# Attention of a two-layer diffusion step: another order for value matmuls, prompt items, inverse sums and modulation chunks

## The reference

```python
def block_attention(q, k, v):
    ...
    def one_block(qi):
        s = jnp.einsum('bqhd,bkhd->bhqk', qi, k).astype(jnp.float32) * scale
        p = jax.nn.softmax(s, axis=-1).astype(v.dtype)
        return jnp.einsum('bhqk,bkhd->bqhd', p, v)
...
def layer_step(x, mod, rope, ctx_ckv, ctx_krope, p):
    sh1, sc1, g1, sh2, sc2, g2 = jnp.split(mod, 6, axis=-1)
    h = rmsnorm(x, p['norm1_g']) * (1 + sc1) + sh1
    mix, ckv, kpe = token_mixers(h, rope, ctx_ckv, ctx_krope, p)
    x = x + g1 * mix
    ...
mod_lat = (jax.nn.silu(c) @ w_ada[l] + b_ada[l])[:, None, :]
```

## Time and profile before

| what | us |
|---|---|
| median of three runs | 2453.25 |
| lowest and highest of them | 2451.75, 2464.22 |
| the profiled execution | 2446.93 |
| its span, first to last instruction | 2445.2 |
| mean granted TensorE clock in it, as a share of full speed | 0.977 |

### The profile page before, as it was taken

How to read it: one execution, slowest core, us unless ns; L and a number is a source line. 1 busy time by engine, 2 the same in 40 slices (tenths; PEclk the granted TensorE clock), 3 DMA queues, 4 the chain that set the end, 5 groups by cost and what they waited for, 6 DMA issues and landing times.

```text
span 2445.2 us, 30291 instructions
## 1 busy us (share of the span) xinstructions
PE 2318.5 (95%) x12256; PEld 1512.7 (62%) x12256; DVE 748.3 (31%) x1419; ACT 508.0 (21%) x1048; POOL 276.9 (11%) x434
## 2 busy tenths in 40 slices
PE   6999989999997999999999999999999969999996
PEld 4545546555445887888754455455554458887884
DVE  2401245553338111111142022545623541111113
ACT  3310122221334101010142102212223320111003
POOL 3000011211001112111210000220100011112111
PEclk8999999999998999999999999999999979999998
DMA  9100169768246888889950001975642268888888
GB/s 335 34 6 16 52 133 248 203 124 233 95 154 224 263 276 271 274 279 287 327 166 17 22 0 52 204 171 114 128 125 103 78 241 275 269 273 283 274 279 296
DMA packets 215864, 440.44 MB, mean 180 GB/s; under 512 B 31936, under 2 KB 75128, under 8 KB 215776
## 3 DMA queue, kind: packets, MB, share of 16 engines
q1 hardware_dynamic: 167920, 358.71, 46.6%
q0 software_dynamic: 22768, 54.29, 9.0%
q10 hardware_dynamic: 25088, 26.23, 4.7%
HBM read 339.08 MB, written 47.65 MB: 158 GB/s over the span
## 4 chain that ended last, share of the span: by engine, by line
PE 77%; issue 7%; DMA 6%; DVE 4%; ACTq 1%; POOL 1%; ACT 1%; SPq 1%; POOLq 0%; DVEq 0%
PE PS L1361 11%; PE PS L1368 11%; PE PS L1207 11%; PE PS L1393 9%; PE PS L991 8%; PE PS L945 6%; PE PS L932 5%; PE PS L1387 2%; PE PS L1084 2%; DMA inv_dram<-oinv 2%; PE PS L1141 2%; ACTq L1587 1%; PE PS L1096 1%; PE PS L1045 1%; DMA r<-ring 1%
## 5 line engine op out<-in xcount | busy, mean ns | idle before, releaser
L1361 PEld LDWEIGHTS PS<-r,ring 128*128 128x128 f32 x2048 | 281.9, 190 | 15.2 <-issue 15.2
L1207 PE MATMUL PS<-ring,mix 128*128 128x512 f32 x640 | 288.4, 598 | 1.2 <-DVE mix L1966 1.2
L1361 PE MATMUL PS<-r,ring 128*128 128x160 f32 x2048 | 284.0, 299 | 0.3 <-ACT r L1687 0.3
L1368 PE MATMUL PS<-r,ring 128*128 128x160 f32 x2048 | 283.4, 299 | 0.0
L1368 PEld LDWEIGHTS PS<-r,ring 128*128 128x128 f32 x2048 | 279.9, 190 | 0.0
L1393 PE MATMUL PS<-ring,r 128*128 128x512 f32 x496 | 221.1, 599 | 0.0
L991 PE MATMUL PS<-r,ring 128*128 128x512 f32 (+1 forms) x576 | 208.4, 521 | 1.6 <-ACT r L1485 1.6
L1084 PE MATMUL PS<-lat,r 128*128 128x512 f32 (+1 forms) x416 | 191.2, 595 | 15.0 <-ACT ring L1550 7.1
L1141 PE MATMUL PS<-r 128*128 128x256 f32 x768 | 183.3, 391 | 15.3 <-DMA r<-ring 9.8
L1207 PEld LDWEIGHTS PS<-ring,mix 128*128 128x128 f32 x640 | 116.4, 190 | 129.7 <-issue 129.7
L1141 PEld LDWEIGHTS PS<-r 128*128 128x128 f32 x768 | 147.4, 195 | 59.9 <-issue 18.0
(11 more groups left out here) (308 smaller groups left out, 2176.1 us busy)
## 6 DMA issues: line engine op xcount, KB each, us to landing
ring<-in_w_gate_dram SPq DMA_DIRECT2D x32, 2048.0 KB
ring<-in_w_up_dram SPq DMA_DIRECT2D x32, 2048.0 KB, 11.6
ring<-in_w_down_dram SPq DMA_DIRECT2D x31, 2048.0 KB, 9.4
ring<-in_w_ada_dram SPq DMA_DIRECT2D x15, 2048.0 KB, 9.9
r<-ring SPq DMA_DIRECT2D x128, 96.0 KB
r<-ring ACTq DMA_DIRECT2D x128, 96.0 KB
r<-r SPq DMA_DIRECT2D x128, 96.0 KB
r<-r ACTq DMA_DIRECT2D x128, 96.0 KB
```

Of the source, the lines that this page charges most:

```text
L1207: ins = pe.matmul(psum(2 * (s % 2) + n, 512), mix[:, k, tile * P:(tile + 1) * P], W_OUT[n][:, k, :], start=(k == 0), stop=(k == KD - 1))
L1361: ins = pe.matmul(PS[:, b // 2, (b % 2) * 256:(b % 2) * 256 + SLOTS], W_G[:, k, b * P:(b + 1) * P], XST[par][:, k, :], start=(k == 0), sto ...
L1368: ins = pe.matmul(PS[:, 2 + b // 2, (b % 2) * 256:(b % 2) * 256 + SLOTS], W_U[:, k, b * P:(b + 1) * P], XST[par][:, k, :], start=(k == 0), ...
```

## The change

Six edits, all in the attention stage and the first steps of the projection:

1. `ITEMS`: both prompt items come last, as items 16 and 17.
2. TensorE's loop: all of `times_values(n - 2)` stands behind the scores of item n. `modulation(n)` follows it, and `turn_modulation(n - 1)` stands behind the first scores of item n. So chunk i belongs to item i, from iteration 0 on.
3. SP: two modulation loads ahead of the first exchange, later ones behind the exchange of the item two before.
4. VectorE's loop: `copy_modulation(n - 1)` first, `divide_out(n - 4)`, `invert_sums(n)` and `bias_modulation(n)` last.
5. `INV`, `oinv` and `inv_dram` have four buffers instead of two, and the last item's inverse goes through DRAM as the others do; `spread_last`, `divide_last` and the matmul with ones are gone. POOL's store for the last item stands behind its loads of the gates.
6. Value heads: eight matmuls of 512 columns for the sample tokens between the last value matmuls, and the four of 256 columns for the prompt tokens (`prompt_value_heads`) in the second step of the projection.

```diff
@@ -45,8 +45,8 @@
 for _p in range(2):
-    ITEMS.append((_p, PROMPT_TILES))
     ITEMS += [(_p, t) for t in range(PT, NT)]
+ITEMS += [(_p, PROMPT_TILES) for _p in range(2)]
...
-        INV = [lat[:, 512 * i:512 * (i + 1)] for i in range(2)]
-        DIAG = lat[:, 1024:1280].rearrange("p (s q) -> p s q", s=2)
+        INV = [lat[:, 512 * i:512 * (i + 1)] for i in range(4)]
...
@@ -530,16 +528,18 @@
+                load_ada(0)
+                load_ada(1)
                 for n in range(NI):
-                    if n < len(ADA_ITEMS[l]):
-                        load_ada(n)
+                    exchange(n, (0, 1))
+                    if n + 2 < len(ADA_ITEMS[l]):
+                        load_ada(n + 2)
...
-                    exchange(n, (0, 1))
@@ -712,21 +712,21 @@
                 def spread_inverses(n):
...
-                    if l + n:
-                        pool.wait_ge(inv_landed, at(l, 16 * (NI - 1), 16 * n))
+                    if n >= 4:
+                        pool.wait_ge(inv_landed, at(l, 16 * NI, 16 * (n - 3)))
...
-                    if n >= 2:
-                        pool.wait_ge(o_divided, at(l, NI, n - 1))
+                    if n >= 4:
+                        pool.wait_ge(o_divided, at(l, NI, n - 3))
...
                 for n in range(NI - 1):
-                    store_gate(n - 2)
+                    store_gate(n)
                     spread_inverses(n)
...
+                spread_inverses(NI - 1)
...
@@ -1144,56 +1145,54 @@
                     for c in range(3):
                         scores(n, 0, c)
-                    modulation(n - 2)
-                    times_values(n - 2, first_half)
+                    turn_modulation(n - 1)
                     if n:
                         pe.wait_ge(exp_done, at(l, 2 * NI, 2 * n))
...
-                    turn_modulation(n - 2)
-                    times_values(n - 2, second_half)
+                    times_values(n - 2, range(12))
+                    modulation(n)
 
                 n = NI - 1
+                pe.wait_ge(o_divided, at(l, NI, 8))
+                value_heads(0)
+                value_heads(1)
                 pe.wait_ge(exp_done, at(l, 2 * NI, 2 * n + 1))
...
+                value_heads(2)
+                value_heads(3)
                 times_values(n - 1, range(12))
                 pe.wait_ge(exp_done, at(l, 2 * NI, 2 * n + 2))
...
                 pe.wait_ge(o_divided, at(l, NI, 12))
+                value_heads(4)
+                value_heads(5)
+                pe.wait_ge(o_divided, at(l, NI, 16))
+                pe.wait_ge(uvh_copied[0], at(l, NU // 2, 1))
                 value_heads(6)
+                pe.wait_ge(uvh_copied[1], at(l, NU // 2, 1))
                 value_heads(7)
...
-                pe.matmul(psum(6, 256), ones[:, :], DIAG, start=True, stop=True).then_inc(inv_summed, 1)
...
                 times_values(n, range(12))
...
@@ -1289,6 +1291,10 @@
                 for s in range(NT):
+                    if s == 1:
+                        pe.wait_ge(o_divided, at(l, NI, NI))
+                        prompt_value_heads(0)
+                        prompt_value_heads(1)
                     project(s, 0, 0)
...
                 for n in range(NI):
-                    bias_modulation(n - 2)
-                    divide_out(n - 3)
+                    copy_modulation(n - 1)
                     row_max(n, 0)
                     row_max(n, 1)
-                    copy_modulation(n - 2)
                     turn_blocks(n, 0)
                     turn_blocks(n, 1)
-                    if n < NI - 1:
-                        invert_sums(n)
+                    divide_out(n - 4)
+                    invert_sums(n)
+                    bias_modulation(n)
```

113 lines of the change are left out of this document (45 added, 68 removed).

## The result

| kernel | median, us | runs | profiled span, us | granted clock | first attention, us | second attention, us |
|---|---|---|---|---|---|---|
| before | 2455.28 | 17 | 2445.2 | 0.977 | 269.2 | 267.5 |
| changed | 2462.69 | 17 | 2460.9 | 0.972 | 271.5 | 272.4 |
| forecast for changed | 2430.5 | | | | 259.2 | 250.4 |

The ratio of changed to before is 1.0038, with a 95% interval of 1.0022 to 1.0054: slower by a little, within 0.5% at the median, and far outside the range of 2417 to 2445 us. An attention is counted, as in the prediction, from its first score matmul to its first output projection. The prediction's 252.6 us for the second holds 2.2 us of prompt value heads that lie behind that end, so 250.4 stands in the table.

The account below looks back on a forecast made before the run. TensorE, 95% busy, was taken as the bound, with time to win only where it stands. Summed stage times gave gains of 7.8 and 14.9 us, 22.7 in all: 2453.25 becomes 2430.5 us, range 2417 to 2445.

Parts of the forecast that it names:

- Values at the end: Attention loop: all value matmuls at the iteration's end give exchanges more time; their waits go, 0 in the full loop.
- all fit into 20.9: Attention loop: exchanges measured at 10.8, 17.8 and 17.9 us land within the 20.9 us from issue to first value matmuls.
- The load order: SP queue: modulation loads have 24.6 us from issue to use, as before; no wait was counted.
- Rival 4: Modulation iterations: DMA backlog from iterations 0 and 1 makes 8 iterations wait; 13 us slower, 2466.5 us; chance 0.07.
- The tail: Each attention's end: two short prompt exchanges; the last takes 12.0 us to land, costing a wait of 3.5 us.
- The wait of 1.5 us: Second prompt iteration: TensorE waits 1.5 us for item 15's exchange, issued at +11.1 and asked for at +22.4.
- rival 2: Tail: gate loads, residual loads and two exchanges meet; last exchange 17.9 us, 5.9 more per layer; gain 8, 2445 us; chance 0.14.
- start-up term: Second attention's start, part of rival 2: the 4.32 us idle there stay, some 3 us.
- The 2.7 us of slow clock: Behind the last exchange's wait in the tail: slower matmuls cost 2.7 us, as 12 instructions took 5.49 instead of 2.75.
- Fill: Iterations 0 and 1, without value matmuls: bound by the bias wait at 12.1 us each, 24.2 together in the first attention.
- prompt heads: Second projection step: the prompt's four value heads of 256 columns move there and still cost 2.2 us.
- last inverse: Going through memory, it lands at about 20 us, is asked for at 31; cost 0, cover 11 us.

Follow-up runs that it names:

- values behind the projection: Changed kernel with the first prompt item's values behind the value heads, the second's behind the first tile's projection, prompt value heads one step later: 2457.46 us, ratio 1.0001.
- both remedies: Changed kernel with modulation chunks two items later, last prompt values behind value heads and first projection, late-modulation weight loads behind the first tile's stores: 2430.59 us, ratio 0.9912.
- half loads: Half of each modulation weight loaded, as many matmuls: 2441.18 us (ratio 0.9941) in the changed kernel, 2444.51 us (0.9946) in the kernel before.
- the chunks' move: Changed kernel with each modulation chunk, its load, turn and bias two items later, and the output weights too: 2445.74 us, ratio 0.9962.

## Why the prediction was wrong

**What bounds the kernel.** Half right. "The middle of the loop is a TensorE queue without gaps" holds: once the backlog is gone the changed kernel has iterations of 15.5 us, from one modulation to the next (418.84 to 434.33 and to 449.82). But with modulation the DMA engines are as full as TensorE, 0.97 by the earlier trace rows, and the prediction put that into a rival instead of into this part. Two resources bound that loop, and an edit that closes gaps of one takes them from the other.

**Values at the end.** In the first attention the slack was enough, and 7.4 us of waits went down to 0.2. In the second it was not: "all fit into 20.9" rests on three exchanges of 10.8 to 17.9 us, and one took 24.3. The sum's larger error is to have counted the removed waits as won. Made alone the edit gave them back ahead of the modulation and the scores, and more (ratio 1.0085).

**The load order, "24.6 us, as before", cost 0.** This is the step that failed first. 24.6 us holds between iterations of 15.5; the first loads of the loop have iterations of 12.1 us between issue and use, and were allowed 16.8, 21.4 and 29.5 us. They took 18.8, 26.1 and 31.5, since the issue itself waited (8.54 us for one bias load) and 20.8 us passed behind it. The prediction put these waits at nothing; they cost 8.7 and 6.3 us, and there are slow matmuls behind them (3.20 and 3.64 us for 1.95).

**Rival 4** had this mechanism at a chance of 0.07: a backlog from iterations 0 and 1, too small to decide by 0.9 us (23.7 against 24.6). Its margin compared a landing time taken from one exchange of the kernel before with an allowance of the steady loop, and neither is that of a load in a queue behind an exchange. It came in part: three waits in the first attention and one in the second, 15.0 us, where the rival had eight and 36 us with the slow clock. The time that it gave, 2466.5 us, is within 4 us of what was measured, but that is luck: it had no tail loss in it.

**The tail.** Mis-sized. The last exchange was put at 12.0 us; it took 15.2 and 18.8, and the one before it, for which the sum has no wait, made TensorE wait 2.89 us in the first attention. The wait of 1.5 us that it has is for the exchange of item 15, and came out as 0.2 and 1.9. The range for it, 10.8 to 17.9, was too short: two exchanges in a row and 2.5 MB of loads were more company than the exchanges had had that the range was taken from, as far as the loads explain it; the stores of inverse sums are the untested rival. That is rival 2's term; its start-up term did not come, as the second attention began with iterations of 12 us. The 2.7 us of slow clock were about right (3.78 us for 1.99, then 8.19 for 7.1). Priced apart, the tail is 9 us (values behind the projection) and, as an estimate, up to the 4.8 us more that this edit lost elsewhere.

**Fill, prompt heads, last inverse.** Right in what they cost: iterations 0 and 1 took 12.0 us each, the prompt's value heads 1.9 us in each projection, and the last division made nobody wait. Its inverse came later than forecast, 28 us behind the loop's end and not 20, so that some 7 us were left of the cover of 11.

**The forecast as a whole.** The kernel with both remedies has a ratio of 0.9912, which is 21.6 us of 2453.8 and close to the 22.7 of the forecast. That closeness is partly luck, since it has another order than the one forecast. The order as it stood is not worth 22.7 us even where the loads don't stand in its way: with half loads it is within the intervals of the old order, and its tail waits 24.1 us for exchanges and ScalarE, where the sum had 10.0 for both attentions. What isn't settled is how the 18 us of the chunks' move share out between the waits (15.0 us in the changed kernel, 3.5 left) and the clock behind them, since each trace is one execution.

## What to carry to other kernels

Before a wait for a transfer is counted as won, read the DMA share of the iterations around it: at 0.97 here it was mostly the transfers' own time, and removing it at one place moved it to the next consumer. Where the share is low and the transfer still doesn't land, look at what else is open. Put the extra loads into the iterations that are long by other work, and not into short first ones of a loop. Work that depends on nothing (a projection of tiles long ready) belongs ahead of the last consumer of the last transfer.

## What the runs showed of the hardware

Where transfers have piled up, issuing one takes the issuing engine time: one bias load of 1 KB held SyncE for 8.54 us (DMA share 1.06 from 370.9 to 381.2), while four of them took 1.43 us in all at the start of the kernel before. A full share alone doesn't do it: at 411.54 in the kernel before four took 1.44 us, with a share of 1.01 from 411 to 414. Whatever stands behind it in that queue starts later by that, so the time from issue to landing understates the delay.

An exchange of a prompt item, 512 KB in runs of 256 bytes, landed only after 15.7 us, the last 7.3 us of it at a DMA share of 0.02. A 2 KB store to DRAM had landed by 0.8 us ahead of it; whether it waited for that was not tested.

TensorE's clock did not fall behind each wait. After 2.02 us idle the modulation still took 1.95 us; after 4.73 us it took 3.20; and after 1.97 us, beginning 17 us behind the end of that long wait, 2.84. The granted clock tells them apart: 1.00 (2.4 GHz) up to the long wait, 0.59 in the 3.2 us behind it, so mostly the lower level of 1.2 GHz, 1.00 again from 386.1 to 399.7, and 0.66 from 401.7 to 404.5. One wait's length alone doesn't price what follows it.
